# Two of the four weight sums of an up pair: VectorE additions or accumulating transfers

## The reference

```python
up = rmsnorm(x, g_ffn) @ w_up            # 1024 x 5632, gate a | value b
a, b = up[..., :D_FF], up[..., D_FF:]    # D_FF = 2816 = 22 tiles of 128
a_ext = jnp.concatenate([conv_hist, a], axis=1)
conv = conv_b + sum(a_ext[:, j:j + T] * conv_w[j] for j in range(3))
x = x + (jax.nn.silu(conv) * b) @ w_down
```

## Time and profile before

| | |
|---|---|
| median of 3 runs | 871.52 us (871.28 to 872.45) |
| the profiled execution | 871.67 us |
| its span, first to last instruction | 869.9 us |
| mean granted clock of TensorE | 0.996 of full speed |
| busy TensorE, VectorE, ScalarE, GpSimd | 95%, 70%, 50%, 16% of the span |

### The profile page before, as it was taken

One profiled execution on the slowest core, in us unless ns is written; L12 is line 12 of the kernel. 1 busy time (PEld: TensorE's weight loads), 2 busy tenths in 40 slices (PEclk: granted clock), 3 DMA queues, 4 the chain that ended last, 5 costly groups with the idle time before them and its releaser, 6 DMA issues.

```text
span 869.9 us, 15501 instructions
## 1 busy us (share of the span) xinstructions
PE 830.6 (95%) x5939; PEld 796.3 (92%) x5939; DVE 604.7 (70%) x1118; ACT 437.2 (50%) x793; POOL 142.1 (16%) x246
## 2 busy tenths in 40 slices
PE   6999999999998999999999989999999999999996
PEld 4898989898996899989999988999999999999995
DVE  2887766677765566565766789998469973699733
ACT  6577667647334554343344444665236652366523
POOL 5016475552000020000001000110001100011100
PEclk9999999999999999999999999999999999999999
DMA  6266433236237443110233113333233323332302
GB/s 213 76 208 164 123 111 109 77 105 206 76 94 288 172 121 120 51 49 21 79 95 90 55 49 105 92 96 109 85 96 84 100 74 94 89 98 86 105 31 110
DMA packets 105141, 91.57 MB, mean 105 GB/s; under 512 B 3008, under 2 KB 96406, under 8 KB 104819
## 3 DMA queue, kind: packets, MB, share of 16 engines
q1 hardware_dynamic: 99939, 73.51, 27.8%
q0 software_dynamic: 5136, 17.17, 6.5%
HBM read 81.32 MB, written 9.35 MB: 104 GB/s over the span
## 4 chain that ended last, share of the span: by engine, by line
PE 77%; DVE 12%; ACT 5%; DMA 3%; issue 2%; POOL 0%; SPq 0%; DVEq 0%; ACTq 0%
PE ps L2700 22%; PE ps L434 20%; PE ps L2710 12%; PE ps L2350 4%; PE ps L2530 3%; PE ps L2243 3%; PE ps L2586 2%; PE ps L2536 1%; PE ps L2615 1%; PE ps L2636 1%; PE ps L2330 1%; DVE w_lo L460 1%; DMA x_tok<-in_x_sample 1%; DMA w_raw<-in_w_mk 1%; PE ps L2373 1%
## 5 line engine op out<-in xcount | busy, mean ns | idle before, releaser
L2700 PE MATMUL ps<-up_lo,slot_hi 128*128 128x288 f32 x504 | 149.1, 296 | 0.0
L2700 PE MATMUL ps<-up_hi,slot_lo 128*128 128x288 f32 x504 | 148.4, 295 | 0.0
L2700 PE MATMUL ps<-up_hi,slot_hi 128*128 128x288 f32 x504 | 148.3, 294 | 0.0
L1077 ACT ACTIVATE slot_hi<-raw 128x512 fp32r<-128x512 f32 (+2 forms) x118 | 64.4, 554 | 83.3 <-PE ps L2710 56.7
L464 DVE TENSOR_TENSOR slot_lo<-raw,slot_hi 128x512 fp32r<-128x512 f32 (+2 forms) x118 | 70.3, 598 | 37.4 <-ACT slot_hi L1077 37.1
L2700 PEld LDWEIGHTS ps<-up_hi,slot_lo 128*128 128x128 f32 x504 | 95.0, 188 | 0.0
L2700 PEld LDWEIGHTS ps<-up_hi,slot_hi 128*128 128x128 f32 x504 | 94.8, 188 | 0.0
L2700 PEld LDWEIGHTS ps<-up_lo,slot_hi 128*128 128x128 f32 x504 | 94.7, 188 | 0.0
L2710 PE MATMUL ps<-part_hi,slot_hi 128*128 128x288 f32 x352 | 76.5, 299 | 8.0 <-DVE part_lo L464 5.6
L2710 PE MATMUL ps<-part_hi,slot_lo 128*128 128x288 f32 x352 | 75.8, 296 | 0.0
L2710 PE MATMUL ps<-part_lo,slot_hi 128*128 128x288 f32 x352 | 75.6, 296 | 0.0
(11 more groups left out here) (408 smaller groups left out, 2075.0 us busy)
## 6 DMA issues: line engine op xcount, KB each, us to landing
raw<-in_w_up SPq DMA_DIRECT2D x36, 512.0 KB, 5.1
raw<-in_w_down SPq DMA_DIRECT2D x12, 768.0 KB, 4.4
w_raw<-in_w_in SPq DMA_DIRECT2D x15, 512.0 KB, 4.0
w_raw<-in_w_o SPq DMA_DIRECT2D x8, 512.0 KB, 4.0
w_raw<-in_w_mq SPq DMA_DIRECT2D x8, 512.0 KB, 4.1
w_raw<-in_w_mo SPq DMA_DIRECT2D x8, 512.0 KB, 4.1
w_raw<-in_w_up SPq DMA_DIRECT2D x8, 512.0 KB, 3.9
w_raw<-in_w_mk SPq DMA_DIRECT2D x6, 512.0 KB, 4.0
```

Of the source, the lines that this page charges most:

```text
L1077: return nc.scalar.activation(out, x, ACT.Copy, scale=scale)
L2700: ins = mm(up_bank(k, e, b), w[g % AHEAD][:, m * P:m * P + P], y[:, m, x], start=(first and m == 0 and w is slot_hi and y is up_hi), stop= ...
```

## The change

The blocks for s1 and s3 are summed on the way in. GpSimd loads, for pair n, the block w10 twice, into the two halves of one of two new buffers `landed_sum`, waits until both are there, and then issues two transfers that add to what lies in the buffer: w11 onto the first half (s1), w00 onto the second (s3). ScalarE and VectorE read factors s1 and s3 from there. VectorE still makes s2 = s1 + w00 and s4 = s2 + w01, in two `row_sum` buffers. SP no longer loads w10, of which only the sums had use. The new buffers lie over `a_hi`, free after the last plain product (`weight_used`, `w_all`); the two semaphores are those of an earlier stage.

The loads for pairs 0 and 1 are issued when the plain products are done. Those for pair n + 2 are issued when GpSimd reaches tile n of the pairs and the low part of pair n's s3 has been taken (`SUM3_LOW`). VectorE waits for the landed sums before its s2, ScalarE before it rounds s1 or s3.

```diff
-        row_sum = [place(f"row_sum{s}", [P, 4 * P]) for s in range(3)]
+        row_sum = [place(f"row_sum{s}", [P, 4 * P]) for s in range(2)]
...
+        here[0] = at["a_hi"]
+        landed_sum = [place(f"landed_sum{c}", [P, 2, 4 * P]) for c in range(2)]
...
-        SUM_HOME = {"s1": 0, "s2": 1, "s3": 2, "s4": 0}
-        SUM_COUNT = {"s1": 1, "s2": 2, "s3": 3, "s4": 4}
+        LANDED_SUM = {"s1": 0, "s3": 1}
+        SUM_HOME = {"s2": 0, "s4": 1}
+        SUM_COUNT = {"s2": 1, "s4": 2}
+        sums_landed, SUMS_BEFORE = [cache_k_landed, cache_v_landed], 16 * PAIRS
...
+        SUM3_LOW = [g + 1 for g, f in enumerate(SLOTS) if f[5] == "s3"]
...
+        def wait_landed_sums(engine, n):
+            engine.wait_ge(sums_landed[n % 2], SUMS_BEFORE + 64 * (n // 2 + 1))
...
-                        sp.dma_start(tile_raw[r % 2][:, :, half * P:half * P + P],
-                                     a["w_up"][0][:, col:col + P].rearrange(cols_k, p=P)).then_inc(raw_landed[r % 2], 16)
+                        sp.dma_start(tile_raw[r % 2][:, half::half + 1, half * P:half * P + P],
+                                     a["w_up"][0][:, col:col + P].rearrange(cols_k, p=P)[:, half::half + 1]).then_inc(raw_landed[r % 2], 16)
...
+            def load_sums(n):
+                if n >= NF - PLAIN:
+                    return
+                buffer, landed, before = landed_sum[n % 2], sums_landed[n % 2], SUMS_BEFORE + 64 * (n // 2)
+                w = a["w_up"][0].rearrange("(m l p) c -> l p m c", l=2, p=P)
+                gates, values = (slice(c + (PLAIN + n) * P, c + (PLAIN + n + 1) * P) for c in (0, DFF))
+                for c in range(2):
+                    pool.dma_start(buffer[:, c].rearrange("p (m c) -> p m c", c=P), w[0, :, :, values]).then_inc(landed, 16)
+                pool.wait_ge(landed, before + 32)
+                for c, (l, cols) in enumerate(((1, values), (0, gates))):
+                    pool.dma_start(buffer[:, c].rearrange("p (m c) -> p m c", c=P), w[l, :, :, cols],
+                                   accum_op=ALU.add).then_inc(landed, 16)
+
             for f in range(NF):
+                if f == PLAIN:
+                    pool.wait_ge(weight_used, w_all)
+                    load_sums(0)
+                    load_sums(1)
+                if f >= PLAIN:
+                    pool.wait_ge(slot_lo_ready, SUM3_LOW[f - PLAIN])
+                    load_sums(f - PLAIN + 2)
                 wait_gate(pool, f)
...
-                    act.wait_ge(row_sums, 4 * up_pair(*SLOTS[g][1:3]) + SUM_COUNT[SLOTS[g][5]])
+                    act.wait_ge(row_sums, 2 * up_pair(*SLOTS[g][1:3]) + SUM_COUNT[SLOTS[g][5]])
+                if SLOTS[g][5] in LANDED_SUM:
+                    wait_landed_sums(act, up_pair(*SLOTS[g][1:3]))
...
-                if name == "s1":
+                if name == "s2":
                     dve.wait_ge(raw_landed[r % 2], landed_count(r))
-                    if n >= 1:
-                        dve.wait_ge(slot_lo_ready, g - 2)
-                if name == "s4":
-                    dve.wait_ge(slot_lo_ready, g - 3)
-                if name in ("s2", "s4"):
-                    dve.wait_ge(row_sums, 4 * n + SUM_COUNT[name] - (1 if name == "s2" else 2))
-                x, y = {"s1": (raw_block(g, 1, 0), raw_block(g, 1, 1)), "s2": (sum_rows("s1"), raw_block(g, 0, 0)),
-                        "s3": (raw_block(g, 0, 0), raw_block(g, 1, 0)), "s4": (sum_rows("s2"), raw_block(g, 0, 1))}[name]
-                nc.vector.tensor_tensor(sum_rows(name), x, y, add).then_inc(row_sums, 1)
+                    wait_landed_sums(dve, n)
+                if n >= 1:
+                    dve.wait_ge(slot_lo_ready, g - 6)
+                dve.wait_ge(row_sums, 2 * n + SUM_COUNT[name] - 1)
+                x, y = ((sum_rows("s1", n), raw_block(g, 0, 0)) if name == "s2"
+                        else (sum_rows("s2", n), raw_block(g, 0, 1)))
+                nc.vector.tensor_tensor(sum_rows(name, n), x, y, add).then_inc(row_sums, 1)
```

More of the change, by code:

```diff
@@ L741, in raw_block, with sum_rows @@
             return x[:, l, i]
-        def sum_rows(name):
-            return row_sum[SUM_HOME[name]][:].rearrange("p (m c) -> p m c", c=P)
+        def sum_rows(name, n):
+            x = landed_sum[n % 2][:, LANDED_SUM[name]] if name in LANDED_SUM else row_sum[SUM_HOME[name]][:]
+            return x.rearrange("p (m c) -> p m c", c=P)
+        def wait_landed_sums(engine, n):
+            engine.wait_ge(sums_landed[n % 2], SUMS_BEFORE + 64 * (n // 2 + 1))
         def factor(g):
             name = SLOTS[g][5]
-            return raw_block(g, int(name[1]), int(name[2])) if name[0] == "w" else sum_rows(name)
+            return raw_block(g, int(name[1]), int(name[2])) if name[0] == "w" else sum_rows(name, up_pair(*SLOTS[g][1:3]))
         def slot(x, g):
```

## The result

The changed kernel takes **910.13 us** (median of 4 runs, 908.82 to 914.26), the kernel before beside it 871.66 (871.28 to 872.45). The ratio is 1.045, interval 1.042 to 1.048: slower by 4.5%, where no measurable difference was forecast. The profiled execution took 914.26 us, its span is 912.5, 42.6 more than before, and the mean granted clock of TensorE is 0.977.

The account below looks back on a forecast made before the run. TensorE, busy 830.6 of 869.9 us and full in the up pairs, was taken as the bound. Profiled 871.67 - 0.47 = 871.2; with the median 0.15 lower, the forecast was 871.1 us, range 869.4 to 885.

Parts of the forecast that it names:

- the 0.47 us at `x_t` in chunk 0: TensorE's wait for `x_t` near 532 us goes when the `row_sum` ahead of it is removed: 0.47 us, the whole gain.
- Rival 1: At VectorE's s2 addition: sums land later than 14.7 us; 898.7 us at the upper bound, about 885 halfway; chance 0.18.
- GpSimd itself is held 5.6 + 2 x 0.80 = 7.2 us ... 9.25 of 11.11 us; it keeps up: GpSimd's work per pair: plain landing and two accumulating issues, 7.2 us; with `a_last` and the small copy 9.25 of 11.11.
- Two accumulating ones: GpSimd's two adding transfers per pair: 5.6 us plus 1.5 for fetching the old value, 7.1 us.
- 17.0 as the upper bound: Landing of a pair's sums: at most 8.5 us for two plain transfers and at most 8.5 for two accumulating ones.
- 14.7 as the limit: In mid-chunk pairs, the sums must land within 14.7 us after 563.13, when GpSimd's small copy ends, or TensorE stops.
- Rival 1's price: At the 17.0 us bound each of 12 tight pairs is 2.3 us longer: 27.6 us in all, 898.7 us.
- Rival 2: VectorE holds up GpSimd's four issues per pair, 2.2 us each; sums land 6.8 us late, about 953 us; chance 0.07.
- Rival 3: VectorE's freed time keeps TensorE's clock up from 510 to 515 us: 1.7 us faster, 869.4 us; chance 0.08.

Follow-up runs that it names:

- the run with the sums of two pairs: Changed kernel in which GpSimd loads only the sums of pairs 0 and 1, which all later pairs reuse; 871.32 us, ratio 0.9993.
- with 5120: Changed kernel with DMA_SCRATCH, the bytes reserved for GpSimd's transfer descriptors, at 5120 instead of 3072; 882.36 us, ratio 1.011.

## Why the prediction was wrong

**What held.** TensorE bounds the pairs, and no time on VectorE freed there is worth anything. The gain is the 0.47 us at `x_t` in chunk 0 (2.3 to 1.9 us of waits), and with next to none of GpSimd's transfers the kernel comes to 871.32 (the run with the sums of two pairs), where 871.1 was forecast. More bytes and the wait for the plain pair cost nothing. Rival 1's place and order were right as well: s2, then `up_b`, then the seventh product, with pairs more than 12 us apart (13.5 to 15.6 between the s2 additions from 554.66 to 598.85).

**The step that failed** is the overlap in "GpSimd itself is held 5.6 + 2 x 0.80 = 7.2 us ... 9.25 of 11.11 us; it keeps up", and with it "Two accumulating ones", taken at 7.1 us for both. Three things in it were wrong:
- The step has both accumulating transfers in flight together. At 3072 the second waits 3.5 us for the first, and plain ones behind them wait too. This is the large one: with 5120 the loss goes from 4.5% to 1.1%. Where there is room, the 7.1 us were about right: with 5120 both are down 6.7 us after the first issue at 559.09 (the second lands 5.9 us after its own, at 559.9). Without it they took 10.1 (570.29 - 560.19).
- An accumulating issue takes 1.30 us, not 0.80: 2.6 for two, 1.0 more. I had taken the price of a plain issue.
- The plain pair takes 7.8 us in the changed kernel (560.19 - 552.41), and 6.7 or 9.0 with 5120, not 5.6.

In the changed kernel the transfers alone hold GpSimd 7.8 + 1.3 + 3.5 + 1.3 = 13.9 us, more than a pair's 11.11. With 5120 it keeps up where the plain pair takes 6.7, and waits 0.77 us for VectorE; with 9.0 the loop is 12.3. Where the accumulation is dropped it holds: 6.6 + 1.5 and 1.7 for the copies are 9.8, and GpSimd waits 1.36 us for VectorE.

The sums' landing came out at 7.8 + 10.1 = 17.9 us where I took 5.6 + 7.1 = 12.7, with 17.0 as the upper bound and 14.7 as the limit (570.17 - 0.29 makes it 14.6): rival 1 at a little more than its bound, in 9 pairs and not 12. A late loop adds up from pair to pair, which my bound, made for one pair alone, left out.

**Rival 1's price** of 898.7 was too small by a term that I had not counted: after the longer waits the granted clock is lower. The idle time is 25.0 us; that it is near its 27.6 is luck, eight waits of 0.69 to 4.67 us in place of twelve of 2.3. TensorE's busy time is 15.7 us more. The earlier trace rows had the pattern, a wait of 2.83 us and 0.66 of the clock after it; I used it only for a gain.

**Rival 2** is refuted. It needs issues of 3 us that depend on VectorE. The 36 accumulating issues of the changed kernel take 1286 to 1325 ns, the 1316 ns at 832.27 beside a VectorE that is busy throughout and the 1303 ns at 837.17 beside one that is busy for 0.08 us of it (columns as in the earlier trace rows):

```profile
832.27:833.59 1.32, 1.32 (x12) 1.32 (x11) 1.32 (x3) 0.63 (x1) 1.31 (x1) 1.00 0.00 0
837.17:838.47 1.30, 1.30 (x12) 1.30 (x11) 0.08 (x1) 0.41 (x1) 1.30 (x4) 1.00 0.87 287
```

Those in the run without addition take 747 to 758. The limit in the Trainium skill, page "SBUF — State Buffer", section "Who interferes with whom", by which an addition with two SBUF inputs does not hold up a GpSimd instruction that reads no SBUF, agrees with that. The longer issue belongs to the kind of transfer.

**Rival 3** is refuted by the run with the sums of two pairs.

**Left open:** how the queue counts its room. The runs show only what fits in 3072, 4096 and 5120; that it goes by packets (528 against 80) fits them, and no run tried it. Open as well: why the plain pair's landing varies, and what the lower clock alone costs.

## What to carry to other kernels

Work given to transfers is still work of the engine that issues them: add up its loop per step (issue times, waits for landing, its other instructions) against the pace of the step, with the prices of that very kind of transfer, and ask whether the queue has room for all that is in flight. Waits marked "issue" in front of a transfer, as long as the previous one's landing, are the sign that it has not, and a larger reservation tells it apart from a slow transfer in one run. Where TensorE stands still for some microseconds, look at the granted clock behind the wait, and count the slower matmuls there too.

## What the runs showed of the hardware

- An accumulating transfer of 256 KB in runs of 512 bytes from GpSimd is 528 packets and 1.30 us of issue; the plain one of the same shape 80 packets and 0.75 to 0.78 us. The Trainium skill, page "DMA: Bandwidth & Descriptors", section "Anatomy of one DMA — SWDGE (gpsimd) path", calls the time to generate a transfer's descriptors small and variable; here the whole issue takes 1.30 us, twice per pair, where a pair lasts 11.11.
- Landing (minimum, median): plain transfers only 3.3 and 3.6 us; with accumulating ones among them 3.2 and 4.7.
- With 3072 bytes reserved, a second accumulating transfer waited until the first had landed; with 4096 it did not.
- After a wait of 3.27 us TensorE's granted clock was 0.62 from 574 to 578 us and 1.00 from 578 to 582; after one of 0.69 us it stayed at 1.00.
